# The value projection of the pooled branch: three passes of rounded parts instead of plain fp32 matmuls

## The reference, cut to what matters

```python
p = jnp.einsum("btd,dn->btn", h, w_in)
a_val, a_glu, a_gate, b_val, b_gate = jnp.split(p, [1024, 2048, 3072, 4096], axis=-1)
u = a_val * jax.nn.sigmoid(a_glu)
u = causal_depthwise_conv(u, conv_w, conv_b)              # 31 taps
u = jax.nn.silu(layernorm(u, ln_g, ln_b))
ya = u * jax.nn.silu(a_gate)
d = multiscale_pool_diff(b_val)                           # windows 2, 4, 8, 16
d = jnp.einsum("btgc,gce->btge", d, pool_w) + pool_b
yb = (d * pool_scale) * jax.nn.silu(b_gate)
y = jnp.concatenate([ya, yb], axis=-1)
return jnp.einsum("btn,nd->btd", y, w_out)
```

## Time and profile before

| what | value |
|---|---|
| device time, median of 3 runs | 1225.47 us (1223.67 to 1226.38) |
| device time of the profiled execution | 1229.22 us |
| its span, first to last instruction | 1227.5 us |
| PE busy | 1108.4 us, 90% of the span |
| DVE busy | 787.1 us, 64% |
| POOL busy | 605.3 us, 49% |
| ACT busy | 547.4 us, 45% |
| mean granted TensorE clock | 0.943 of full |

### The profile page before, as it was taken

One profiled execution on the slowest core, in us unless ns is written; L12 is line 12 of the kernel. 1 busy time (PEld: TensorE's weight loads), 2 busy tenths in 40 slices (PEclk: granted clock), 3 DMA queues, 4 the chain that ended last, 5 costly groups with the idle time before them and its releaser, 6 DMA issues. The chain is left out here.

```text
span 1227.5 us, 21138 instructions
## 1 busy us (share of the span) xinstructions
PE 1108.4 (90%) x8017; PEld 1021.3 (83%) x8017; DVE 787.1 (64%) x1470; ACT 547.4 (45%) x1054; POOL 605.3 (49%) x470
## 2 busy tenths in 40 slices
PE   5999789999999999989989999989988879776886
PEld 5899777888889887879979999979987768765886
DVE  6568778787763279873455542237997694555954
ACT  3355446766564013444345543333333353466331
POOL 5356134554544024865443443365784654633661
PEclk8999889999999999979989999989998998888889
DMA  6334222333224322315435555534543333323331
GB/s 245 114 122 150 73 87 104 105 119 116 93 104 146 129 104 86 104 68 177 167 121 176 186 187 174 175 118 172 172 139 122 119 120 120 120 95 113 107 134 69
DMA packets 42581, 158.07 MB, mean 129 GB/s; under 512 B 4848, under 2 KB 4848, under 8 KB 41968
## 3 DMA queue, kind: packets, MB, share of 16 engines
q1 hardware_dynamic: 42192, 155.64, 36.4%
q10 hardware_dynamic: 288, 1.08, 0.2%
HBM read 155.65 MB, written 1.05 MB: 128 GB/s over the span
## 5 line engine op out<-in xcount | busy, mean ns | idle before, releaser
L1615 PE MATMUL p_proj<-arena_r,ring_hi 128*128 128x256 f32 x2080 | 636.8, 306 | 66.7 <-issue 34.6
L1616 PE MATMUL p_proj<-arena_r,ring_hi 128*128 128x256 f32 x2080 | 605.4, 291 | 0.0
L1617 PE MATMUL p_proj<-arena_r,ring_lo 128*128 128x256 f32 x2080 | 604.7, 291 | 0.0
L467 POOL TENSOR_TENSOR ring_lo<-ring,ring_hi 128x1024 fp32r<-128x1024 f32 x174 | 419.8, 2416 | 331.3 <-ACT ring_hi L791 330.8
L1615 PEld LDWEIGHTS p_proj<-arena_r,ring_hi 128*128 128x128 f32 x2080 | 413.9, 199 | 95.7 <-issue 55.9
L1616 PEld LDWEIGHTS p_proj<-arena_r,ring_hi 128*128 128x128 f32 x2080 | 416.6, 200 | 6.3 <-issue 5.0
L1617 PEld LDWEIGHTS p_proj<-arena_r,ring_lo 128*128 128x128 f32 x2080 | 416.3, 200 | 0.0
L791 ACT ACTIVATE ring_hi<-ring 128x1024 fp32r<-128x1024 f32 x260 | 273.1, 1052 | 125.9 <-PE p_proj L1617 117.8
L467 DVE TENSOR_TENSOR ring_lo<-ring,ring_hi 128x1024 fp32r<-128x1024 f32 x86 | 112.3, 1306 | 84.9 <-ACT ring_hi L791 83.6
L1604 PE MATMUL p_proj<-arena,ring 128*128 128x256 f32 x464 | 115.1, 399 | 19.7 <-issue 10.7
L1604 PEld LDWEIGHTS p_proj<-arena,ring 128*128 128x128 f32 x464 | 88.8, 199 | 38.3 <-issue 21.8
(11 more groups left out here) (257 smaller groups left out, 1197.4 us busy)
## 6 DMA issues: line engine op xcount, KB each, us to landing
ring<-w_stream SPq DMA_DIRECT2D x289, 512.0 KB, 3.2
arena<-w_tok SPq DMA_DIRECT2D x1, 1632.0 KB, 13.0
arena<-x_t SPq DMA_DIRECT2D x1, 1024.0 KB, 5.5
arena<-w_cmp ACTq DMA_DIRECT2D x1, 1024.0 KB, 8.7
out_t<-arena SPq DMA_DIRECT2D x1, 1024.0 KB, 3.9
par<-cols SPq DMA_DIRECT2D x1, 323.0 KB, 8.1
row<-rows ACTq DMA_DIRECT2D x1, 32.0 KB, 5.6
```

The source lines that it names most:

```text
L467: return eng.tensor_tensor(ring_lo[:, u % RING, :, :].rearrange("p k n -> p (k n)"), ring[:, u % RING, :, :].rearrange("p k n -> p (k n)") ...
L1615: pe.matmul(slot(s)[:, 0:S], w_hi, hi, start=(c == 0), stop=False)
L1616: pe.matmul(slot(s)[:, 0:S], w_hi, lo, start=False, stop=False)
L1617: mm = pe.matmul(slot(s)[:, 0:S], w_lo, hi, start=False, stop=(c == n - 1))
```

## The change

`b_val` leaves the set of plain names, and the branch that gave it the unsplit input goes:

```diff
-PLAIN = {"br_dsa", "br_nsa", "b_val", "pool", "rg_ig"}
+PLAIN = {"br_dsa", "br_nsa", "pool", "rg_ig"}
...
-                    elif name == "b_val":
-                        rhs = [A(HF + c) for c in range(8)]
```

## The result

| | before | changed |
|---|---|---|
| device time, median (4 runs each, same chip) | 1224.87 us | 1237.45 us |
| lowest to highest | 1223.67 to 1226.38 | 1236.51 to 1239.49 |
| ratio to before, 95% interval | | 1.0096 (1.0076 to 1.0117) |
| profiled execution | 1229.22 us | 1236.51 us |
| its span | 1227.5 us | 1234.8 us |

The change makes the kernel slower by 12.6 us (9.3 to 14.3 by the interval). The forecast was 1235.5 us, with a range of 1229.5 to 1239.5.

A forecast was written before the change was run, and what follows sets the result against it. PE was taken to bound the b_val stretch, with DVE as good as full. The job saving of 4.7 us was already inside a net +10.4, rounded to +10, on 1225.47: 1235.5 us, range 1229.5 to 1239.5.

The forecast's parts named there:

- What the jobs save: b_val jobs, 834 to 891 us: each falls from 3.46 to 2.87 us, eight times, -4.7 us on PE.
- ACT, B0, DMA at nothing: Eight ACT copies and the first b_val subtraction, ahead of the convolution, cost nothing; no DMA is added.
- B1: Second b_val job: subtraction behind econv 1 on DVE, weights at 845.0 us, PE standing still 3.8 to 5.6 us.
- The clock: PE behind a stall such as that at the second b_val job: slow clock costs 0 to 1.9 us more.
- B4: the mis-sized term: Fifth b_val job, subtraction behind econv 8: PE waits again, job ends at 876.1 us against 868.15, bounds 872.1 and 878.0.
- POOL's chain: POOL, fifth b_val job's window sum to G0's weights: 33.9 us of work, weights 10.4 us later, bounds 6.4 and 12.3.
- To the end: From G0 on: DVE stays at or before PE, so both shift by the same 10.4 us.
- The gain kept: b_val stretch: added subtractions ready in time, POOL's work fits its idle time; 1224.2 to 1220.8 us, chance 0.05.
- DVE's length alone: b_val stretch: PE's stalls are made up, only DVE's longer queue counts; +2.4 to +5.7 us, chance 0.12.
- More slow clock: Jobs behind every new stall run at 1.2 GHz, 1.9 us each beyond the forecast; +13 to +16 us, chance 0.08.

The follow-up runs named there:

- Without subtractions: The change with its eight b_val subtractions left out, the third matmul rereading the rounded weights: -3.3 us against the kernel before.
- the run with B1 alone: Only the b_val job B1 split, its subtraction on DVE, the other seven plain as in the kernel before: +1.8 us against that kernel.
- the window sums: The change in full, with each window sum on POOL three jobs later: +9.9 us against the kernel before.
- the run one step earlier: The change with DVE's b_val subtractions moved to right behind the previous job's place in DVE's list: +6.4 us against the kernel before.

## Why the prediction was right

The direction, the size and, as far as G0, the mechanism held; behind G0 it was incomplete. By its own steps:

1. *What the jobs save.* A split b_val job is 2.88 us where nothing waits, forecast 2.87. Without subtractions 3.3 us of the 4.7 arrive.
2. *ACT, B0, DMA at nothing.* Held: the mixer's first evictions came within 0.2 us of before, and B0's subtraction ran in DVE's idle time. B2 and B3, also at nothing, brought one wait of 0.4 us at V8.
3. *B1.* Forecast: DVE waits out POOL's second subtraction, weights at 845.0, PE stands for up to 5.6 us. Measured 844.1 (all times 0.9 earlier in this execution) and 5.61. That this meeting is open to both outcomes, 1.23 or 2.86 us, the run with B1 alone showed, where DVE came half a microsecond sooner; I had taken it as settled by arithmetic.
4. *The clock.* Held: 0.50 behind B1's wait. B1 took 849.50 - 844.25 = 5.25 us, above my bound of 4.8, which came from G0; more of it lay in the slow clock, which was 0.50 until 849.0.
5. *B4: the mis-sized term.* Counted from the stage's start, B4's end came at 64.5 us, before 54.3: +10.2, where I took +8.0 and at most +9.9. I had shifted econv 8 by B1's subtraction alone, by 3.2 us at most, and it shifted by 5.0. Line 1257 ahead of it also reads two SBUF operands, and its two instructions took 3.13 us, beside a subtraction and a window sum of POOL's, where the same pair took 1.31 before (at 862.07). B4's own subtraction took 1.70 (forecast 2.4), PE waited 2.6 us, and the job took 4.8 us (forecast 3.9).
6. *POOL's chain.* From B4's window sum to G0's weights I added up 33.9 us; it took 910.14 + 2.4 - 878.21 = 34.3. This sum was the best of the prediction, since no wait was left in it but 0.5 us.
7. *To the end.* G0 + 12.9 us in the stage, the layer norm +12.4, the time +12.6, forecast +10: the difference is the 2.2 us of point 5 and the 0.4 of point 6. The reason that I gave, that DVE stays ahead, is true at G0 (8.5 us of wait) but incomplete. DVE's own queue was 5.7 us longer by then (free at 909.1 in this execution, 96.1 into the stage, against 90.4), and that with luck: the next pair of line 1257 took 1.20 us at 897.68, where before it took 3.77. So undoing PE's delay alone wouldn't have given the time back, as the window sums showed.

*The rivals.* The gain kept: refuted, B1 was to start before 841.9, and started at 844.25 + 0.9 = 845.1 on the clock of the execution before. DVE's length alone: refuted as the whole cause by the waits and by the run one step earlier, but it is the second bound. More slow clock: in part, B1, B4 and B6 ran slowly, and G0 as before; V14 didn't. On the rule of the Trainium skill ("SBUF — State Buffer", "SBUF: two separate sides"), that the pair of ports is locked exclusively: both orders were seen, DVE 2.86 with POOL 4.65, and DVE 1.23 with POOL 5.72. It raised my sum to the right side.

*What stays open.* How the +12.4 divides between POOL's chain and DVE's lengthening behind G0, and why the kernel with B1 alone is +4.8 in its profile's stage and +1.8 by its median. One profile for each kernel doesn't tell a chance meeting of DVE and POOL from the rule, and so it is open too how much of the window sums' gain belongs to the order.

## What to carry to other kernels

An operation that PE waits for should not be queued behind work that its engine does at leisure: in this kernel three subtractions of 1.2 us inside a convolution without a break cost some 10 us (the fourth, ahead of it, ran in idle time), and eight of 2.4 us on an engine with gaps cost 2.5. Price an inserted step by when its engine gets to it, not by its length, and then follow what starts late behind it. And before a cheaper operation is put in, look for the work that can go later: moving the window sums, with no operation changed, brought 5.3 us in one version and 2.3 in another, where three passes with free remainders brought 3.3. The intervals of these overlap, so which brings more is not shown.

## What the runs showed of the hardware

The timeline of PE in the changed kernel, at B1's first passes behind the wait and where the clock rises again:

```profile
844.25 0.55 PE L1613 MATMUL p_proj<-arena_r,ring_hi 128*128 128x256 f32 x1 [5.61 <-DVE ring_lo L467]
844.60 0.41 PE L1614 MATMUL p_proj<-arena_r,ring_hi 128*128 128x256 f32 x1
844.81 0.41 PE L1615 MATMUL p_proj<-arena_r,ring_lo 128*128 128x256 f32 x1
845.02 0.41 PE L1613 MATMUL p_proj<-arena_r,ring_hi 128*128 128x256 f32 x1
...
848.86 0.36 PE L1613 MATMUL p_proj<-arena_r,ring_hi 128*128 128x256 f32 x1
849.06 0.28 PE L1614 MATMUL p_proj<-arena_r,ring_hi 128*128 128x256 f32 x1
849.18 0.28 PE L1615 MATMUL p_proj<-arena_r,ring_lo 128*128 128x256 f32 x1
```

- A block of 128 x 128 by 256 columns takes 2.88 / 24 = 0.12 us a pass in rounded form at 2.4 GHz, so 0.36 us for three; the plain fp32 one takes 3.46 / 8 = 0.43 us as two records. At 1.2 GHz a rounded pass takes 0.21 us, by the starts of the rows above: not twice but 1.8 times as long.
- A subtraction on DVE of 128 x 1024 took 1.23 to 2.86 us in the changed kernel, and up to 3.21 one step earlier (at 861.26), by what POOL was doing, and one on POOL a microsecond more when it met DVE's. Which of the two waits changed from kernel to kernel. A pair of line 1257 on DVE, 0.41 us each at best, took 0.76 us in one kernel and 4.95 in another (all subtractions on POOL, at 891.29).
- The slow clock behind a wait of 5.6 us lasted until 849.0, so a job of 2.88 us took 5.25. Behind waits of 1.6 and 1.9 us (V14, B6) the jobs took 907.05 - 902.30 - 1.6 = 3.1 and 896.23 - 890.01 - 1.9 = 4.3 us.
